# A Mixture-of-Experts encoder layer: the order of one block's work on TensorE, ScalarE and VectorE

## The reference

```
scores = sigmoid(u @ router_w);  idx = top_k(scores + router_b, 8)
wts    = 2.5 * scores[idx] / sum(scores[idx])
for each expert e and its tokens:
    g, up = split(u[tokens] @ w_gu[e])      # 1024 -> 2 x 256
    y     = (silu(g) * up) @ w_down[e]      # 256 -> 1024
    out[tokens] += wts * y
out += swiglu(u, shared_w_gu, shared_w_down)
```

## Time and profile before

| | us |
|---|---|
| median of 3 runs | 1511.7 |
| lowest, highest | 1511.02, 1514.17 |
| the profiled execution | 1509.93 |
| its span, first to last instruction | 1508.2 |
| mean granted TensorE clock | 0.962 of full speed |
| loop: first and last turn of h | 701.94, 1425.81 |

### The profile page before, as it was taken

How to read it: one execution, slowest core, us unless ns; L and a number is a source line. 1 busy time by engine, 2 the same in 40 slices (tenths; PEclk the granted TensorE clock), 3 DMA queues, 4 the chain that set the end, 5 groups by cost and what they waited for, 6 DMA issues and landing times.

```text
span 1508.2 us, 27517 instructions
## 1 busy us (share of the span) xinstructions
PE 1357.9 (90%) x5830; PEld 986.7 (65%) x5831; DVE 896.2 (59%) x1407; ACT 636.8 (42%) x795; POOL 193.3 (13%) x322
## 2 busy tenths in 40 slices
PE   1599999569999997887999999999999999999955
PEld 0278886358888885654677767676777776776722
DVE  4721445986534587665776566776676655555428
ACT  2272216323323221324665465665565554454301
POOL 0000000000000000121222122222221222322200
PEclk9999999789999998989999999999999999999978
DMA  9411301114233675435897687998798766576185
GB/s 307 153 60 56 112 1 56 56 56 138 86 112 113 214 253 196 153 127 174 311 346 265 227 297 249 328 358 273 274 348 305 261 238 242 189 282 213 69 342 192
DMA packets 105867, 302.80 MB, mean 201 GB/s; under 512 B 21642, under 2 KB 24914, under 8 KB 96739
## 3 DMA queue, kind: packets, MB, share of 16 engines
q1 hardware_dynamic: 77168, 255.88, 48.8%
q0 software_dynamic: 20800, 33.61, 6.4%
q10 hardware_dynamic: 7858, 12.79, 2.4%
HBM read 321.07 MB, written 40.90 MB: 240 GB/s over the span
## 4 chain that ended last, share of the span: by engine, by line
PE 59%; DVE 16%; DMA 9%; issue 5%; ACT 4%; DVEq 3%; ACTq 3%; SPq 0%
PE psum L1379 24%; PE psum L1549 16%; PE psum L1590 9%; DMA gu_raw<-in_exp_w_gu 8%; PE psum L1539 3%; DVE gu_lo L1240 2%; ACT gu_hi L842 2%; DVE tmp_tok L1016 2%; PE psum L1446 1%; PE psum L1437 1%; DVEq L1235 1%; DVEq L1237 1%; PE psum L1579 1%; PE psum L1354 1%; PE psum L1488 1%
## 5 line engine op out<-in xcount | busy, mean ns | idle before, releaser
L1240 DVE TENSOR_TENSOR gu_lo<-gu_raw,gu_hi 128x1024 f32 x212 | 250.3, 1221 | 85.4 <-ACT gu_hi L842 63.8
L842 ACT ACTIVATE gu_hi<-gu_raw 128x1024 f32 x212 | 219.8, 1056 | 112.0 <-issue 56.7
L1590 PE MATMUL psum<-w_dn,mask 128*128 x560 | 251.6, 592 | 0.0
L1549 PE MATMUL psum<-gu_hi,xT_hi 128*128 (+1 forms) x568 | 228.3, 402 | 3.6 <-DVE xT_lo L1230 2.9
L1549 PE MATMUL psum<-gu_hi,xT_lo 128*128 (+1 forms) x568 | 222.2, 391 | 0.0
L1549 PE MATMUL psum<-gu_lo,xT_hi 128*128 (+1 forms) x568 | 222.1, 391 | 0.0
L1590 PEld LDWEIGHTS psum<-w_dn,mask 128*128 128x128 f32 x560 | 106.1, 189 | 105.9 <-issue 100.5
L1379 PE MATMUL psum<-uT_hi,w_hi 128*128 128x512 f32 x352 | 139.1, 395 | 13.3 <-DVE w_lo L420 12.2
L420 DVE TENSOR_TENSOR w_lo<-ring,w_hi 128x1024 fp32r<-128x1024 f32 x80 | 95.2, 1222 | 94.0 <-ACT w_hi L413 91.9
L413 ACT ACTIVATE w_hi<-ring 128x1024 fp32r<-128x1024 f32 x80 | 82.5, 1058 | 134.6 <-PE psum L1379 61.7
L1379 PE MATMUL psum<-uT_lo,w_hi 128*128 128x512 f32 x352 | 138.1, 392 | 0.0
(11 more groups left out here) (283 smaller groups left out, 1983.5 us busy)
## 6 DMA issues: line engine op xcount, KB each, us to landing
gu_raw<-in_exp_w_gu SPq DMA_DIRECT2D x212, 512.0 KB, 6.3
w_dn<-in_exp_w_down SPq DMA_DIRECT2D x70, 1024.0 KB
ring<-in_w_in SPq DMA_DIRECT2D x56, 512.0 KB, 5.2
ring<-in_ada_w SPq DMA_DIRECT2D x48, 512.0 KB, 4.7
ring<-expert_rows SPq DMA_DIRECT2D x8, 1024.0 KB, 8.7
ring<-in_w_branch_b SPq DMA_DIRECT2D x8, 512.0 KB, 5.5
ring<-in_w_branch_a SPq DMA_DIRECT2D x8, 512.0 KB, 5.4
ring<-in_w_out SPq DMA_DIRECT2D x8, 512.0 KB, 5.3
```

The source lines that it names most:

```text
L842: act.activation(gu_of(gu_hi, order, p), gu_raw[:, PK * p:PK * p + PK], ACT.Copy).then_inc(gu_hi_ready, 1)
L1240: tt(gu_of(gu_lo, order, p), gu_raw[:, PK * p:PK * p + PK], gu_of(gu_hi, order, p).bitcast(F32), ALU.subtract).then_inc(gu_split, 1)
L1549: mm = pe.matmul(moe_bank(GU), rows[:, s % 2, k], w[:, bass.ds(order % 2, 1), k].rearrange("p o n -> p (o n)"), start=(k == 0 and m == 0), ...
L1590: mm = pe.matmul(moe_bank(Y0 + g), hT[:, j], w_dn[:, bass.ds(order % 3, 1), j, g * NC:(g + 1) * NC].rearrange("p o n -> p (o n)"), start=( ...
```

## The change

In each step of the loop, three engines change their order; nothing else is changed, and the part in front of the loop is as it was. On TensorE `gate_up(b+1)` comes directly behind the turn of h, and `find` and `turn_rows` come behind it, ahead of the down product. On ScalarE `rows_hi(b+2)` comes behind the fourth piece of `expert_hi(b+2)`. On VectorE `find_rows`, `rows_lo` and `pick_rows` come behind the fourth piece of `expert_lo(b+2)`.

```diff
@@ ScalarE
                 act.activation(hT..., moe_bank(HT)[:, 0:2 * P], ACT.Copy).then_inc(hT_ready, 1)
-                rows_hi(b + 2, s)
                 expert_hi(b + 2, range(PIECES - 1))
                 silu(b + 1)
                 expert_hi(b + 2, (PIECES - 1,))
+                rows_hi(b + 2, s)
@@ VectorE
                 dve.wait_ge(add_ready, b + 1)
+                expert_lo(b + 2, range(PIECES - 1))
+                gated_up(b + 1)
+                expert_lo(b + 2, (PIECES - 1,))
                 find_rows(b + AHEAD, s)
                 rows_lo(b + 2, s)
                 pick_rows(b + AHEAD + 1)
-                expert_lo(b + 2, range(PIECES - 1))
-                gated_up(b + 1)
-                expert_lo(b + 2, (PIECES - 1,))
@@ TensorE
                 mm.then_inc(hT_psum, 1)
+                gate_up(b + 1, s + 1, after)
                 find(b + AHEAD)
                 turn_rows(b + 2, (s + 2) % UNROLL, 16 * (i + (s + 2) // UNROLL) + 16)
-                gate_up(b + 1, s + 1, after)
```

## The result

The changed kernel takes 1577.87 us (median of 4 runs, 1574.22 to 1579.26) against 1511.74 before (1511.02 to 1514.17, 4 runs). The ratio is 1.043, with a 95% interval of 1.041 to 1.045: slower by 66 us. Forecast were 1564, with a range of 1543 to 1586.

A forecast was written before the change was run, and what follows sets the result against it. TensorE, busy 99.85 of 100 us, was taken as the bound. First step 12.6, 50 x 11.38 and 18 x 10.32 make 767.4 against 716.3; with +1.0 at the end, +52: 1562 profiled, 1564 median, range 1543 to 1586.

The forecast's parts named there:

- The mechanism: On TensorE, gate/up was to wait for `rows_lo` some 50 times, 50 to 60 us, with no turn of h waiting for `gated_up`.
- two kinds: Loop steps were to take 11.4 us where block b+2 brings a new expert and 10.3 where it doesn't.
- The chain's terms: From gate_up(b+1)'s start G over silu, fourth piece, `find_rows` and `rows_lo` to gate_up(b+2): 11.38 us, 1.06 beyond TensorE's 10.32.
- Steps without a fresh expert: Loop steps whose block b+2 brings no new expert: 10.32 us, no stall, with 0.1 added for the down product's weight load.
- The register loads: On ScalarE, `expert_hi`'s loads were taken to cost 1.09 us behind silu; the skill's queue rule would hide them under silu's wait.
- First step: The loop's first step was put at 12.6 us, with 1.2 for a colder start of TensorE.
- usual fresh steps: Steps where block b+2 brings a new expert, 51 in the loop; put at 11.38 us each behind the first step.
- The tail behind the last product: Behind gate_up(70) the last down product also has find and turn ahead of it: +1.0 us.
- rival 2: TensorE's clock falls after idling before gate/up products: 15 to 60 us on top, about 1600; 3 in 100.
- Rival 1: The rows' chain fits beside the products, 10.29 us under 10.32, with the register loads hidden: -2 us, 1510; 5 in 100.
- Rival 3: The fourth raw piece's DMA reload lands later than 8.9 us and lengthens steps: +25 us, so 1590; 4 in 100.

The follow-up runs named there:

- Experiment 3: Changed kernel with `rows_lo` put ahead of `find_rows` on VectorE: 1567.64 us, ratio 1.035 to the kernel before.
- Experiment 4: Changed kernel with the fourth piece on ScalarE reusing the registers loaded for the first three: 1542.92 us, ratio 1.019 to the kernel before.
- experiment 2: Kernel before with only TensorE in the new order, ScalarE and VectorE in the old: 1942.88 us, ratio 1.283.
- experiment 10: Kernel before with the fourth piece reusing the registers on both ScalarE and VectorE: 1512.03 us, ratio 0.998.
- experiments 3 to 10: Eight runs: seven edits of the changed kernel in register loads, `rows_lo` order or place of the fourth piece, and one of the kernel before; 1512.03 to 1567.64 us.
- experiment 11: Kernel before with one register load for all pieces on both engines, VectorE's set between `find_rows` and `rows_lo`: 1499.9 us, ratio 0.990.
- experiment 5: Changed kernel with the fourth piece reusing registers on ScalarE and VectorE, and `rows_lo` ahead of `find_rows`: 1534.83 us, ratio 1.013.
- experiments 6 to 9: Changed kernel with registers shared on both engines (1523.34 us), or four pieces ahead of silu (1522.7), plus `rows_lo` first (1532.09), plus `pick_rows`' register loaded early (1522.56).
- experiment 1: Changed kernel with TensorE's part put back, so only ScalarE and VectorE take the new order: 1706.09 us, ratio 1.128.
- experiment 6: Changed kernel with the fourth piece reusing registers on both ScalarE and VectorE, `find_rows` still first: 1523.34 us, ratio 1.006.

## Why the prediction was right

**The mechanism.** The wait, its place and its number came as forecast: gate/up on `rows_lo`, 52 waits of 58.0 us, where "some 50 times and 50 to 60 us" stood. Steps fall in two kinds. None of the waits for `gated_up` is left. The clock is the exception, below.

**The chain's terms.** Forecast and measured (G = 921.68): silu 5.75 and 5.77; fourth high piece 7.23 and 7.24; fourth low piece 8.52 and 8.53; `find_rows` 9.66 and 9.68; `rows_lo` 9.96 and 9.96; next product 11.38 and 11.48. Only the last seam was off: from the end of `rows_lo` to the first matmul it is 0.29 to 0.30, not the 0.19 of the earlier trace rows. Experiment 3 took a small term out, and the usual step fell by its full 0.3. Experiment 4 took out 1.17, and the step fell by 0.59, since VectorE's own loads came to bind.

**Steps without a fresh expert.** 10.26 on average of 18, forecast 10.32. That is 0.05 over the 10.21 of before, where I had added 0.1 for the down product's weight load. So TensorE's new order is nearly free in a step where nothing stalls.

**The register loads.** Experiment 4 decides between the two: taking the loads out moved the fourth piece 1.17 us nearer to silu. The chain that ended last names them in the step above (L835 and L837 are the two `value_load`s):
```profile
927.45 0.28 ACT sel L849
...
928.14 0.28 ACTq L837
...
928.92 1.07 ACT gu_hi L842
```
The Trainium skill's picture of engine instructions waiting in a queue while the sequencer reads on (Advanced Engine Details and Errata, Sequencer and Instruction Queues) does not hold here for the loads behind silu's wait: the first began with silu, at 927.5. It does hold in experiment 2, where silu stands behind three pieces of 2.95 us and finds the product long done: the same loads ran at 883.6 to 884.7, under the pieces, and the fourth piece followed silu without a gap (886.31). What in the wait holds the sequencer isn't shown.

**Where the sum was short.** The profiled execution took 1578.0, forecast 1562: 16 us, in these terms:
- Before the loop: the first product starts at 712.78 instead of 710.78, 2.0. In the other kernels here, whose part in front of the loop is the same, it starts between 710.7 and 716.5 (716.5 in experiment 10, which has the old order), so this is scatter and no effect of the change.
- First step: 14.1 instead of 12.6, 1.5. The product ran its first 12 or so matmuls at the 1.2 GHz level (0.50 in the window from 712.7 to 718); I had allowed for half of that.
- 44 usual fresh steps: 11.52 on average instead of 11.38, 6.2.
- Six further fresh steps: 11.8, 12.0, 12.3, 12.4 and twice 13.2 instead of 11.38, 6.6.
- 18 others: 1.1 less. The tail behind the last product: 0.9 more.

Sum 16.1. The term that was put at nothing is the long fresh steps. The kernel before already had such stalls: its 69 steps take 716.3, 11.8 more than 69 of 10.21, and the sum gave the new kernel none. Its two longest are the steps that begin with `gate_up(17)` and `gate_up(33)` (11.75 and 11.36), the same two that take 12.3 and 12.4 here. In experiments 3 to 10 they are 0.8 us or more over the usual fresh step as well; only in experiment 11 they take 10.21.

The two steps of 13.2 are rival 2, with 3 chances in 100, in a small part of the loop. The first of them, on TensorE, and the window of its slow part:
```profile
908.50 0.49 PE L1549 MATMUL psum<-gu_hi,xT_hi 128*128 x1 [1.81 <-DVE xT_lo L1230]
...
909.52 0.62 PE L1549 MATMUL psum<-gu_lo,xT_hi 128*128 x1
909.94 0.63 PE L1549 MATMUL psum<-gu_hi,xT_lo 128*128 x1
```
```profile
909.50:912.90 3.40, 3.40 (x9) 2.62 (x8) 1.49 (x4) 2.37 (x3) 0.85 (x1) 0.50 1.01 310
```
TensorE had stood idle for 1.81 us. Its clock went to 0.50, the 1.2 GHz level, for some eight matmuls, 0.43 us apart instead of 0.23, and silu came at G + 7.38 instead of 5.77: 1.6 us, twice. Behind idle times of 1.0 to 1.54 us in this trace it never happened, nor behind the 1.26 of the earlier trace rows. The idle time alone doesn't decide it: in experiment 5 three products stood behind 2.0 us, and one of them (at 1066.61) ran slow. The long idle time itself begins with a gap of 1.95 us marked "issue" ahead of `row_w` on VectorE, at 896 and again near 1080 us, with gaps of 1.0 marked the same on ScalarE. Their cause wasn't tried.

Rival 1 (the chain fits) came near to true only when I made it so, in experiments 6 to 9, with usual fresh steps of 10.3 to 10.6, and even there the time stayed 0.6 to 1.1% above the kernel before. Rival 3 didn't come: in all 51 fresh steps the fourth high piece is held up by "issue", in none by a transfer.

## What to carry to other kernels

When a stage is moved behind another on one engine, write down the loop from the product back to itself over all engines, with every register load that stands behind a wait; the loop is the step if it is longer than the bound engine's own work. Count the stages queued ahead of the instruction too, not only its own waits (experiment 1). And before reordering a loop whose main engine is at 99%, look for register loads in bare places of a helper engine's loop: sharing them between the pieces and moving them into an existing wait was worth 1%, and the reorder cost 4%.

## What the runs showed of the hardware that I had not expected

- Two register loads behind a wait cost 1.17 us on ScalarE (fourth piece at G + 7.24 or 6.07; the comparison and branch stand in both), and one load costs 0.72 us on VectorE where only small instructions stand in front of it. Behind `rows_lo` of 1.22 us the one load isn't seen (experiment 6), behind three pieces of 2.95 us the two aren't (experiment 2).
- An idle time of 1.81 us on TensorE was followed by 8 matmuls at the 1.2 GHz level, those of 1.0 to 1.54 us in the same trace by none, and two of the three of 2.0 us in experiment 5 by none. In experiment 2, with 256.1 us of idle time in front of 69 turns, the longest 4.8, the mean clock of a stretch was 0.83.
- The seam from VectorE's last half to the first matmul is 0.19 us in the earlier trace rows and 0.29 in the changed kernel. Why it differs is open.
